# Weight chunks of a decoder trunk on their way to bf16: half-size casting loads held behind x, eight DRAM to DRAM conversions for four, no zero columns, half of the direct casts stored one period later

## The chip, the cores and the metric

The kernel runs on all 8 cores of one Trainium2 chip, each core with its own sequence of the batch and no traffic between cores. The metric is the device time in microseconds (us) of the slowest core. The weights are the same for all cores and each core converts and loads its own copy.

## The reference, cut to what matters

One layer: `h = x + W_out[concat(HGRN2(n), SWA(n))]` with `n = RMSNorm(x)`, then `h + SqReLU-MLP(RMSNorm(h))`, then a final RMSNorm, for 8 prompts of 4096 tokens and 128 samples of 8 tokens.

```python
zq, zf, zi, zg, sq, sk, sv = _split(xn @ w_in)          # 1024 -> 4*512 | 512, 128, 128
o_hg, S_new = _hgrn2(zq, zf, zi, zg, lb, hg_norm, S0)    # chunked linear recurrence, 4 heads of 128
o_swa, k_buf, v_buf = _swa_prompt(q, k, v, sinks)        # window of 128, 8 query heads, 2 kv heads
h = h + jnp.concatenate([o_hg, o_swa], axis=-1) @ w_out  # 1024 -> 1024
u = _rmsnorm(h, ln_mlp) @ w_up                           # 1024 -> 4096
h = h + jnp.square(jax.nn.relu(u)) @ w_down              # 4096 -> 1024
```

Inputs and weights are float32, matmuls run in bf16. So every weight has to be cast once and has to be on the core again for each group of tokens.

## The kernel before

**Groups and periods.** A core has 32 tiles of 128 tokens, in 8 groups of 4 tiles, and 16 samples of 8 tokens that ride along with group 3. For each group there is a *head* (`head_steps`, the input projections), a *back* (`back_steps`: recurrence and window attention, then the output projection and the norm of the MLP) and the MLP (`mlp_steps`). `interleave` weaves them: while the MLP of group g runs (a *period*), the back of group g+1 and the head of group g+2 are issued between its matmuls. Before the first period comes an opening: the head of group 0 (`head_steps` with `take=hold_on`), and then a *bridge*, in which `interleave("p", ...)` weaves the head of group 1 (on the buffers `A`) with the back of group 0.

**Weights.** The host packs the weights into 24 chunks of 1024 x 512, `wall` in DRAM (float32, 2 MB each). Chunk 0 is q, 1 is g, 2 is f, 3 the window queries s, 4 is v, 5 holds keys and values of the window attention in 256 columns and zeros in the other 256; 6 and 7 are W_out, 8 to 15 W_up, 16 to 23 W_down. On the core a chunk lies in one of five SBUF slots (`wring`, s_wr in the profile, 1 MB of bf16). `WORDER` is the order in which the slots are filled; it comes from two dry builds of the program and is `2 0 1 3 4 5 2 6 7 8 9 16 20 10 11 6 7 17 21 12 13 18 22 14 15 2 19 0 23 1 3 4 5 8 9 ...`. `w_prefetch` fills a slot as soon as it is released in the program's order; `w_load` does one load.

**The ways of a chunk.** All of them are DMAs:

- a *direct cast*, s_wr<-wall on the POOL queue, which reads float32 and writes bf16 into the slot;
- a *store*, wbf<-s_wr on the SP queue, which saves the bf16 chunk to DRAM (`wbf`) after a direct cast. `tick`, called at each step of the weaving, issues it ten steps or more later, or `w_load` does when the slot or the chunk is wanted;
- a *read*, s_wr<-wbf on the SP queue, 1 MB, for every later use;
- a *conversion*, wbf<-wall on the POOL queue, DRAM to DRAM, which `convert` issues during the bridge (`qc["conv"]`) every `tk["every"]` ticks for the next chunk of WORDER that isn't converted, at most two in flight, and each only when PE has reached the place of its issue.

SP and POOL work their queues in program order: a waiting DMA holds up all DMAs behind it. A direct cast waits until the cast before the last has landed (`casts[-2:-1]`); the first two wait instead for the tiles named in `hold_back`. In the head of group 0 the slots of chunks 0, 1, 3, 4 and 5 are held for the head of group 1; only the slot of f is released, and chunk 5 goes into it, once f is stored.

**The opening's order.** SP: four x tiles of group 0; then a wait for the third cast (`casts[2]`), four x tiles of group 1 (XR<-x); then the stores. `second_norms` makes the norms of group 1's tiles (`norm_pre` L554 to L565 on ACT and DVE, `norm_post` L572 transposes on PE and L574 on DVE); it is pulled, as `beside`, by the sections s and v of the head of group 0.

**Lines of the profile.** L583 is `fm_mm` (projections and W_up), L590 `tm_mm` (v and kv), L572 the transposes, L739 and L753 `hg_front`, L796 to L802 the recurrence, L830 and L855 the window attention, L881 its scores, L1011 the output projection, L1159 to L1181 the MLP's activation and W_down. L621, L627, L637 and L644 are ACT's ends of the projections (tanh, silu, copies), L888 the softmax's exp. L117 is the one line that issues every DMA, L73 the one line of every wait.

```python
for sec in order:                                  # head_steps, "fqgsvk"
    W, u = take(cid)
    ...
                        if beside is not None and sec == "s":
                            next(beside, None)
```

Of the kernel before, what the change touches and what calls it, by code (L numbers as in the profile page):

```python
# [14 lines left out]
G = 4  # L15
# [32 lines left out]
class Prog:  # L48
# [16 lines left out]
    def _wait(self, e, tok):  # L65
        if tok is None:
            return
        sn, v = tok
        if e is self.E["pe"] and sn == "e_pe":
            return  # L70
        if e.waited.get(sn, 0) >= v:
            return
        e.h.wait_ge(self.sems[sn], v)  # L73
        e.waited[sn] = v
# [92 lines left out]
def build_program(worder=None, weights=None):  # L167
# [193 lines left out]
    hold_back = []  # L361
    qc = {"conv": False}

    def store(one):
        cid, s_ = one[0], one[1]
        P.dma(wbf_d[cid], wring[s_].ap.rearrange("p a b -> p (a b)"), reads=[wring[s_]], writes=[wbfb[cid]],
              sem="ws%d" % s_)

# [4 lines left out]
    def w_load(l):  # L373
        cid = WORDER[l]
        for t_ in [t_ for t_ in stores if wslot_free[0] == t_[1] or t_[0] == cid]:
            stores.remove(t_)
            store(t_)
        s_ = wslot_free.pop(0)
        loaded[l] = s_
        dst = wring[s_].ap.rearrange("p a b -> p (a b)")  # L380
        if cid in converted:
            P.dma(dst, wbf_d[cid], reads=[wbfb[cid]], writes=[wring[s_]], sem="wr%d" % s_)
        else:
            converted.add(cid)
            e = P.E["pool"]
            for tok in [hold_back.pop(0)] if hold_back else casts[-2:-1]:
                P._wait(e, tok)
            casts.append(P.dma(dst, wall_d[cid], writes=[wring[s_]], sem="wc%d" % s_, q="pool"))
            stores.append([cid, s_, 10])

# [219 lines left out]
    def head_steps(parts, order="fqgsvk", take=w_use, give=w_release, beside=None):  # L610
# [55 lines left out]
        for sec in order:  # L666
            cid = cids[sec]
            W, u = take(cid)
            if sec in "fqgs":
                for h in range(4):  # L670
                    for B, _, _ in parts:
                        if sec == "f":
                            proj_f(W, B, h)
                        elif sec == "s":
                            proj_l(W, B, h)
                            half_gate()
                        else:
                            proj_s(W, B, h, B.qtT if sec == "q" else B.sgT)
                        if beside is not None and sec == "s":
                            next(beside, None)  # L680
                        yield W_DENSE * B.TB / 512
            elif sec == "v":
                for B, tiles, _ in parts:
                    for j, n in enumerate(tiles):
                        proj_v(W, B, j)
                        half_gate()
                        if beside is not None:
                            next(beside, None)
                        yield W_DENSE
            else:  # L690
                for B, tiles, _ in parts:
# [3 lines left out]
                    for j, n in enumerate(tiles):  # L695
                        proj_kv(W, B, j, n)
                        half_gate()
                        yield W_DENSE / 2
            past.add(sec)
# [543 lines left out]
    def main_schedule():  # L1243
# [73 lines left out]
        const_loads()  # L1317
        hold_back.extend([xs[0][0].w, xs[0][G - 1].w])
        const_ops()
# [3 lines left out]
        if casts:  # L1323
            w_prefetch(1)
            P._wait(P.E["sp"], casts[2])
        xs[1] = [load_x(n) for n in gtiles(1)]
        w_prefetch()
        xbs = []
# [22 lines left out]
        qc["conv"] = True  # L1351
        tk["every"] = 16
        tails = []
        given = []

        def give_up(u):
# [4 lines left out]
                                   take=lambda cid: held.pop(cid) if cid in held else w_use(cid), give=give_up),  # L1361
                   chain(back(0, iter(()), tails, lambda: len(given) >= 3), start_tail(tails)), 4, pace=1.25)
        qc["conv"] = False
        xq.extend([xt_load(xahead.pop(0)), xt_load(xahead.pop(0))])
        for g in range(NG):
# [80 lines left out]
```

How the kernel before makes its waits and increments, by code:

```python
    def _wait(self, e, tok):  # L65
        if tok is None:
            return
        sn, v = tok
        if e is self.E["pe"] and sn == "e_pe":
            return
        if e.waited.get(sn, 0) >= v:
            return
        e.h.wait_ge(self.sems[sn], v)
        e.waited[sn] = v
# [23 lines left out]
    def op(self, en, fns, reads=(), writes=()):  # L98
        e = self.E[en]
        if callable(fns):
            fns = [fns]
        self._deps(e, reads, writes)
        ins = None
        for f in fns:
            ins = f(e.h)
        ins.then_inc(self.sems[e.semname], 1)
        e.n += 1
        tok = (e.semname, e.n)
        self._mark(tok, reads, writes)
        return tok
# [1 line left out]
    def dma(self, out, in_, reads=(), writes=(), sem=None, q="sp"):  # L112
        e = self.E[q]
        sem = sem + "_" + q
        self.dsem(sem)
        self._deps(e, reads, writes)
        ins = e.h.dma_start(out=out, in_=in_)
        ins.then_inc(self.sems[sem], 16)
        self.dcnt[sem] += 16
        tok = (sem, self.dcnt[sem])
        self._mark(tok, reads, writes)
        return tok
```

## Time and profile before

| | us |
|---|---|
| median of 3 runs | 1644.03 |
| their lowest and highest | 1642.82, 1649.74 |
| the profiled execution's own time | 1645.24 |
| its span, core 4 (the slowest) | 1644.2 |
| its spans, all cores | 1628.2 to 1644.2 |

| engine | busy, share of the span |
|---|---|
| PE | 1514.3 us, 92% |
| ACT | 916.0 us, 56% |
| DVE | 736.8 us, 45% |
| POOL | 79.6 us, 5% |

The profile is of one execution on core 4. A matmul's row tells its own duration, about 0.38 us for 512 columns, and matmuls overlap in the pipeline: a group of 8 takes 1.73 us at the full clock. PEclk is the granted share of TensorE's full clock (2.4 GHz; 0.5 is the level of 1.2 GHz). "DMA share" is the mean busy share of the core's 16 DMA engines. The DMA queues: SP's are q1, POOL's q0, ACT's q10.

### The profile page before, as it was taken

To read this page: it belongs to the slowest core of one execution; us is meant where nothing else is said; L and a number is where in the kernel's file an instruction comes from. 1 tells how busy PE (TensorE), PEld (TensorE's weight loads), DVE (VectorE), ACT (ScalarE), POOL (GpSimd) and SP (SyncE) were. 2 spreads that over 40 slices of the span, in tenths; PEclk is the share of its full clock that TensorE was granted. 3 is DMA by queue.
4 is the path that set the end of the run, shared out by engine and by line. 5 is a ranking of instruction groups with operands and counts; after the bars stand their busy time and mean duration, and the time that the engine had idled before them with its cause. 6 is when DMAs were issued, how large, how long until landed. Compare 5 with 4: busy or idle time off the path is not lost.

```text
span 1644.2 us, 26297 instructions; the slowest of 8 cores (1628.2 to 1644.2 us)
## 1 busy us (share of the span) xinstructions
PE 1514.3 (92%) x8883; PEld 737.8 (45%) x8883; DVE 736.8 (45%) x1221; ACT 916.0 (56%) x1694; POOL 79.6 (5%) x154
## 2 busy tenths in 40 slices
PE   4778789899999988999999999999999999999997
PEld 2343344444444544444555544444445444444443
DVE  2545445335542546753544425553544425444222
ACT  3565545556557555546754576555655566444423
POOL 2000000000001001100000000000000000000000
PEclk9999999999999999999999999999999999999998
DMA  8965999966447266633633347734563345534541
GB/s 159 241 131 110 189 235 216 228 220 240 148 151 189 107 234 199 225 128 130 230 129 141 116 154 203 267 120 148 173 254 132 123 152 206 186 129 162 203 154 51
DMA packets 59362, 284.17 MB, mean 173 GB/s; under 512 B 10304, under 2 KB 19520, under 8 KB 32576
## 3 DMA queue, kind: packets, MB, share of 16 engines
q1 hardware_dynamic: 30400, 206.98, 36.7%
q0 software_dynamic: 19520, 70.26, 18.3%
q10 hardware_dynamic: 9312, 5.26, 1.2%
q8 instruction: 75, 1.23, 0.3%
q14 instruction: 55, 0.45, 0.1%
HBM read 265.69 MB, written 49.15 MB: 191 GB/s over the span
## 4 chain that ended last, share of the span: by engine, by line
PE 69%; DMA 12%; ACT 8%; DVE 5%; issue 5%; ACTq 0%; DVEq 0%; SPq 0%; POOL 0%; POOLq 0%
PE pb L583 32%; PE pb L1177 23%; PE pb L1011 6%; DMA s_wr<-wall 5%; DMA s_wr<-wbf 4%; PE pb L590 2%; ACT s_xnb L554 2%; ACT s_rl L1159 2%; PE pb L572 1%; DVE XR L1181 1%; DMA ss<-M 1%; DVE U L718 1%; DMA XR<-x 1%; PE pb L830 1%; PE pb L881 1%
## 5 line engine op out<-in xcount | busy, mean ns | idle before, releaser
L583 PE MATMUL pb<-s_hnT,s_wr 128*128 128x512 bf16 x2184 | 508.0, 382 | 14.4 <-DMA s_wr<-wbf 6.2
L1177 PE MATMUL pb<-s_wr,s_aT 128*128 128x512 bf16 x2048 | 476.7, 381 | 19.2 <-ACT s_aT L1162 15.5
L583 PEld LDWEIGHTS pb<-s_hnT,s_wr 128*128 128x128 bf16 x2184 | 207.9, 98 | 253.8 <-issue 29.6
L1177 PEld LDWEIGHTS pb<-s_wr,s_aT 128*128 128x128 bf16 x2048 | 194.7, 98 | 255.2 <-issue 44.0
L1181 DVE TENSOR_TENSOR XR<-pb,XR 128x512 f32<-128x512 f32 x256 | 175.5, 688 | 198.3 <-PE pb L1177 194.3
L1159 ACT ACTIVATE s_rl<-pb 128x512 bf16<-128x512 f32 (+1 forms) x288 | 159.8, 555 | 174.0 <-PE pb L583 170.6
L583 PE MATMUL pb<-s_xnT,s_wr 128*128 128x512 bf16 x952 | 223.8, 388 | 19.9 <-DMA s_wr<-wbf 11.4
L1162 ACT ACTIVATE s_aT<-s_rl 128x512 bf16<-128x512 bf16 x256 | 161.2, 630 | 24.4 <-ACT s_rl L1159 1.1
L583 PEld LDWEIGHTS pb<-s_xnT,s_wr 128*128 128x128 bf16 x952 | 92.9, 99 | 131.4 <-issue 31.2
L1011 PE MATMUL pb<-s_wr,s_omT 128*128 128x512 bf16 x512 | 123.2, 385 | 5.2 <-DMA s_wr<-wbf 4.2
L554 ACT ACTIVATE s_xnb<-XR 128x1024 bf16<-128x1024 f32 x72 | 75.9, 1054 | 90.3 <-DVE XR L1181 64.1
L565 DVE SCALAR_TENSOR_TENSOR s_xnb<-XR,s_rs,s_gmlp 128x1024 bf16<-128x1024 f32 x32 | 41.1, 1283 | 124.0 <-ACT s_rs L558 124.0
L888 ACT ACTIVATE U<-pb 128x512 bf16<-128x512 f32 x126 | 67.8, 590 | 38.7 <-PE pb L881 37.4
L1011 PEld LDWEIGHTS pb<-s_wr,s_omT 128*128 128x128 bf16 x512 | 50.0, 99 | 65.1 <-issue 8.6
L1201 DVE SCALAR_TENSOR_TENSOR XR<-XR,s_rs,s_gfin 128x1024 f32<-128x1024 f32 x32 | 41.1, 1285 | 81.9 <-ACT s_rs L558 79.5
L1014 DVE TENSOR_TENSOR XR<-pb,XR 128x512 f32<-128x512 f32 x64 | 44.0, 688 | 71.2 <-PE pb L1011 70.6
L572 PE MATMUL pb<-s_ident,s_xnb 128*128 128x128 bf16 x528 | 42.0, 225 | 35.2 <-DVE s_xnb L565 34.5
L590 PE MATMUL pb<-s_wr,s_xnT 128*128 128x512 bf16 (+2 forms) x448 | 65.4, 304 | 0.0
L565 DVE SCALAR_TENSOR_TENSOR s_xnb<-s_xt,s_rs,s_gmix 128x1024 bf16<-128x1024 f32 x25 | 32.1, 1284 | 67.5 <-ACT s_rs L558 67.5
L572 PEld LDWEIGHTS pb<-s_ident,s_xnb 128*128 128x128 bf16 x528 | 35.5, 100 | 51.3 <-issue 39.8
L117 POOL DMA_DIRECT2D y<-XR x32 | 17.3, 542 | 774.3 <-DVE XR L1201 423.1
L627 ACT ACTIVATE U<-pb 128x512 bf16<-128x512 f32 x56 | 33.2, 597 | 37.1 <-PE pb L583 36.1
(201 smaller groups left out, 1379.9 us busy)
## 6 DMA issues: line engine op xcount, KB each, us to landing
s_wr<-wbf SPq DMA_DIRECT2D x167, 1024.0 KB, 5.6
s_wr<-wall POOLq DMA_DIRECT2D x20, 1024.0 KB, 15.1
wbf<-s_wr SPq DMA_DIRECT2D x20, 1024.0 KB, 12.9
y<-XR POOLq DMA_DIRECT2D x32, 512.0 KB, 3.5
s_xt<-x POOLq DMA_DIRECT2D x20, 512.0 KB, 5.9
XR<-x POOLq DMA_DIRECT2D x20, 512.0 KB, 11.8
XR<-x SPq DMA_DIRECT2D x12, 512.0 KB, 10.6
wbf<-wall POOLq DMA_DIRECT2D x4, 1024.0 KB, 13.1
```

The lines of the kernel that those rows point to most:

```text
L554: P.op("act", lambda e: e.activation(out=scrap[:, :], in_=src[:, :], func=AF.Square, accum_out=ssq[:, 0:1]), reads=[src], writes=[ssq, scrap])
L565: P.op("dve", lambda e: e.scalar_tensor_tensor(out=xb[:, :], in0=src[:, :], scalar=rs[:, 0:1], in1=gain[:, :], op0=ALU.mult, op1=ALU.mult) ...
L572: P.op("pe", [lambda e, k=k: e.transpose(bkb[:, k * 128:(k + 1) * 128], xb[:, k * 128:(k + 1) * 128], C.ident[:, :]) for k in range(8)], r ...
L583: P.op("pe", [lambda e, k=k: e.matmul(bk[0:ncols, 0:TB], lhsT=W[:, k, col0:col0 + ncols], rhs=srcT[:, k, 0:TB], start=(k == 0), stop=(k == ...
L590: P.op("pe", [lambda e, k=k: e.matmul(bk[:, 0:ncols], lhsT=srcT[:, k, j * 128:(j + 1) * 128], rhs=W[:, k, c0:c0 + ncols], start=(k == 0), ...
L888: P.op("act", lambda e, pt=pt, bk=bk: e.activation(out=pt[:, :], in_=bk[:, :], func=AF.Exp, scale=0.125), reads=[bk], writes=[pt])
L1011: P.op("pe", [lambda e, k=k: e.matmul(bk[:, :], lhsT=B.omT[:, k, j * 128:(j + 1) * 128], rhs=W[:, k, :], start=(k == 0), stop=(k == 7)) fo ...
L1014: P.op("dve", lambda e: e.tensor_tensor(out=xs_[:, nh * 512:(nh + 1) * 512], in0=bk[:, :], in1=xs_[:, nh * 512:(nh + 1) * 512], op=ALU.add ...
L1159: P.op("act", lambda e, bk=bk, rl=rl, TB=TB: e.activation(out=rl[:, 0:TB], in_=bk[:, 0:TB], func=AF.Relu), reads=[bk], writes=[rl])
L1162: P.op("act", lambda e, fl=fl, rl=rl, TB=TB, B=B: e.activation(out=B.aT[:, fl, 0:TB], in_=rl[:, 0:TB], func=AF.Square), reads=[rl], writes ...
L1177: P.op("pe", [lambda e, f=f, B=B, j=j, W=W, bk=bk: e.matmul(bk[:, :], lhsT=B.aT[:, f, j * 128:(j + 1) * 128], rhs=W[:, f, :], start=(f == ...
L1181: P.op("dve", lambda e, nh=nh, bk=bk, xs_=xs_: e.tensor_tensor(out=xs_[:, nh * 512:(nh + 1) * 512], in0=bk[:, :], in1=xs_[:, nh * 512:(nh ...
```

## The change

It has these parts.

1. A direct cast is made as two DMAs of half a chunk each (rows 0 to 3 and 4 to 7 of the 8 blocks of 128). Each half waits until the half before the last has landed. A slot's reader waits for both halves (`_wait` takes a token of four parts).
2. The first half of the first cast waits for x tile 2 and the second half for x tile 3, where the first cast waited for tile 0 and the second cast for tile 3.
3. All five first casts are issued before group 1's x tiles, and SP waits for `casts[8]`, the first half of the fifth cast, before these tiles, not for the third cast.
4. Chunk 5 is cast, stored and read with its 256 used columns alone (`cut`), in runs of 256 elements.
5. `second_norms` is pulled in section k, once per tile, not in s and v.
6. The bridge has a lead of 0, not 4, and a conversion every 9 ticks, not 16: eight conversions for four (chunks 6, 7, 8, 9, 16, 20, 10, 11 for 6, 7, 8, 9).
7. After the bridge (`qc["thin"]`) every second direct cast isn't stored. Its chunk is cast directly once more in the next period, and stored then. There are ten first casts in the first period (of chunks 17, 21, 12, 13, 18, 22, 14, 15, 19, 23), where there were fourteen; 17, 12, 18, 14 and 19 are cast again in the second.

```diff
@@ -65,6 +65,9 @@
     def _wait(self, e, tok):
         if tok is None:
             return
+        if len(tok) > 2:
+            self._wait(e, tok[0:2])
+            tok = tok[2:]
         sn, v = tok
@@ -377,16 +380,32 @@
         s_ = wslot_free.pop(0)
         loaded[l] = s_
-        dst = wring[s_].ap.rearrange("p a b -> p (a b)")
         if cid in converted:
-            P.dma(dst, wbf_d[cid], reads=[wbfb[cid]], writes=[wring[s_]], sem="wr%d" % s_)
-        else:
-            converted.add(cid)
-            e = P.E["pool"]
+            P.dma(flat(wring[s_], cid), rows(wbf_d, cid), reads=[wbfb[cid]], writes=[wring[s_]], sem="wr%d" % s_)
+            return
+        e = P.E["pool"]
+        for half in range(2):
             for tok in [hold_back.pop(0)] if hold_back else casts[-2:-1]:
                 P._wait(e, tok)
-            casts.append(P.dma(dst, wall_d[cid], writes=[wring[s_]], sem="wc%d" % s_, q="pool"))
-            stores.append([cid, s_, 10])
+            casts.append(P.dma(flat(wring[s_], cid, half), rows(wall_d, cid, half), writes=[wring[s_]] if half == 0 else [],
+                               sem="wc%d_%d" % (s_, half), q="pool"))
+        wring[s_].w = casts[-2] + casts[-1]
+        if qc["thin"] and cid not in once and len(once) % 2 == 0:
+            once.append(cid)
+            return
+        once.append(cid)
+        converted.add(cid)
+        stores.append([cid, s_, 10])
+
+    def cut(ap, cid, half):
+        v = ap[:, 0:8, 0:256] if cid == 5 else ap
+        return v if half is None else v[:, 4 * half:4 * half + 4, :]
+
+    def flat(buf, cid, half=None):
+        return cut(buf.ap, cid, half)
+
+    def rows(dram, cid, half=None):
+        return cut(dram[cid].rearrange("p (a b) -> p a b", a=8), cid, half)
@@ -676,16 +695,12 @@
                             proj_s(W, B, h, B.qtT if sec == "q" else B.sgT)
-                        if beside is not None and sec == "s":
-                            next(beside, None)
                         yield W_DENSE * B.TB / 512
...
                         proj_v(W, B, j)
                         half_gate()
-                        if beside is not None:
-                            next(beside, None)
                         yield W_DENSE
@@ -695,6 +710,8 @@
                         proj_kv(W, B, j, n)
                         half_gate()
+                        if beside is not None:
+                            next(beside, None)
                         yield W_DENSE / 2
@@ -1315,16 +1332,15 @@
-        hold_back.extend([xs[0][0].w, xs[0][G - 1].w])
+        hold_back.extend([xs[0][G - 2].w, xs[0][G - 1].w])
         const_ops()
         w_prefetch(1)
         const_masks()
         w_prefetch(1)
         if casts:
-            w_prefetch(1)
-            P._wait(P.E["sp"], casts[2])
+            w_prefetch()
+            P._wait(P.E["sp"], casts[8])
         xs[1] = [load_x(n) for n in gtiles(1)]
-        w_prefetch()
@@ -1349,7 +1365,7 @@
         qc["conv"] = True
-        tk["every"] = 16
+        tk["every"] = 9
@@ -1359,8 +1375,9 @@
         interleave("p", head_steps([(A, gtiles(1), None)], order="qgsfvk",
                                    take=lambda cid: held.pop(cid) if cid in held else w_use(cid), give=give_up),
-                   chain(back(0, iter(()), tails, lambda: len(given) >= 3), start_tail(tails)), 4, pace=1.25)
+                   chain(back(0, iter(()), tails, lambda: len(given) >= 3), start_tail(tails)), 0, pace=1.25)
         qc["conv"] = False
+        qc["thin"] = True
```

What moves on the engines can't be read from the diff at three places. In what follows s_hnT is the buffer in which group 1's norms lie during the bridge, pb a PSUM bank. The first place is PE at the end of the head of group 0 and the start of the bridge. Before:

```order
L590 MATMUL pb<-s_wr,s_xnT 128x512 x8
L572 MATMUL pb<-s_ident,s_xnb 128x128 x8
L590 MATMUL pb<-s_wr,s_xnT 128x512 x24
L583 MATMUL pb<-s_xnT,s_wr 128x512 x8
L590 MATMUL pb<-s_wr,s_xnT 128x128 x32
L583 MATMUL pb<-s_hnT,s_wr 128x512 x32
L739 MATMUL pb<-U 128x128 x4
```

Now (lines are 16 to 19 higher: L602 is the old L583, L609 the old L590, L591 the old L572, L756 the old L739):

```order
L609 MATMUL pb<-s_wr,s_xnT 128x512 x32
L602 MATMUL pb<-s_xnT,s_wr 128x512 x8
L609 MATMUL pb<-s_wr,s_xnT 128x128 x16
L591 MATMUL pb<-s_ident,s_xnb 128x128 x8
L609 MATMUL pb<-s_wr,s_xnT 128x128 x8
L591 MATMUL pb<-s_ident,s_xnb 128x128 x8
L609 MATMUL pb<-s_wr,s_xnT 128x128 x8
L591 MATMUL pb<-s_ident,s_xnb 128x128 x16
L756 MATMUL pb<-U 128x128 x4
L770 MATMUL pb<-s_ident,U 128x128 x4
L602 MATMUL pb<-s_hnT,s_wr 128x512 x8
```

All four transposes of group 1 now stand behind the key projection, and the first recurrence step stands ahead of the q projection of group 1 (32 matmuls), not behind it.

The second place is the POOL queue from the fifth cast to the first cast of the first period. wc, ws, wr and cd are the semaphores of casts, stores, reads and conversions, with the slot's number; e_pe is PE's progress. Before:

```order
L117 DMA s_wr4<-wall 128x4096 [waits wc2_pool]
L117 DMA s_wr0<-wall 128x4096 [waits wc3_pool,e_pe,ws0_sp]
L117 DMA wbf<-wall 32x16384 [waits e_pe] x2
L117 DMA wbf<-wall 32x16384 [waits e_pe,cd0_pool]
L117 DMA wbf<-wall 32x16384 [waits e_pe,cd1_pool]
L117 DMA s_wr3<-wall 128x4096 [waits wc4_pool,wr3_sp,e_pe]
```

Now:

```order
L120 DMA s_wr4<-wall 128x2048 [waits wc3_0_pool]
L120 DMA s_wr4<-wall 128x2048 [waits wc3_1_pool]
L120 DMA s_wr0<-wall 128x4x256 [waits wc4_0_pool,e_pe,ws0_sp]
L120 DMA s_wr0<-wall 128x4x256 [waits wc4_1_pool]
L120 DMA wbf<-wall 32x16384 [waits e_pe] x2
L120 DMA wbf<-wall 32x16384 [waits e_pe,cd0_pool]
L120 DMA wbf<-wall 32x16384 [waits e_pe,cd1_pool]
```

The last two of these rows come three times each in a row, eight conversions in all, and the next direct cast is that of chunk 17, far into the first period. Chunk 5's cast waits for the store of f (ws0) as before.

The third place is the SP queue behind that store. Before:

```order
L117 DMA s_wr1<-wbf 128x4096 [waits cd0_pool,wr1_sp,e_pe]
L117 DMA s_wr2<-wbf 128x4096 [waits cd1_pool,wr2_sp,e_pe]
L117 DMA wbf<-s_wr3 128x4096 [waits e_pe,wc3_pool]
L117 DMA s_xt0<-x 128x1024
L117 DMA s_xt1<-x 128x1024
L117 DMA wbf<-s_wr4 128x4096 [waits e_pe,wc4_pool]
L117 DMA wbf<-s_wr0 128x4096 [waits e_pe,wc0_pool]
L117 DMA s_wr2<-wbf 128x4096 [waits wr2_sp]
```

Now:

```order
L120 DMA s_wr1<-wbf 128x4096 [waits cd0_pool,wr1_sp,e_pe]
L120 DMA s_wr2<-wbf 128x4096 [waits cd1_pool,wr2_sp,e_pe]
L120 DMA s_wr3<-wbf 128x4096 [waits cd0_pool,wr3_sp,e_pe]
L120 DMA s_wr4<-wbf 128x4096 [waits cd1_pool,e_pe,ws4_sp]
L120 DMA s_wr0<-wbf 128x4096 [waits cd0_pool,e_pe,ws0_sp]
L120 DMA s_xt0<-x 128x1024
L120 DMA s_xt1<-x 128x1024
L120 DMA s_wr1<-wbf 128x4096 [waits cd1_pool,wr1_sp,e_pe]
```

Both pieces begin with the reads of chunks 8 and 9. The four chunks behind them (16, 20, 10, 11) were direct casts with stores, and are now reads of 1 MB that wait for their conversions, and there is no store among them.

## Rows read from the trace of the kernel before

**Rows 1.** The page, chain that ended last, by line, whole span

```profile
PE pb L583 32%; PE pb L1177 23%; PE pb L1011 6%; DMA s_wr<-wall 5%; DMA s_wr<-wbf 4%; PE pb L590 2%; ACT s_xnb L554 2%; ACT s_rl L1159 2%; PE pb L572 1%; DVE XR L1181 1%; DMA ss<-M 1%; DVE U L718 1%; DMA XR<-x 1%; PE pb L830 1%; PE pb L881 1%
```

**Rows 2.** Windows: length; busy of PE, PEld, DVE, ACT, POOL; clock; DMA share; GB/s

```profile
89.00:146.00 57.00, 41.65 (x294) 21.03 (x293) 28.66 (x62) 41.40 (x61) 1.51 (x3) 0.91 0.64 121
...
172.00:212.00 40.00, 33.46 (x185) 15.56 (x183) 18.42 (x32) 20.58 (x39) 1.06 (x2) 0.91 1.01 219
212.00:317.00 105.00, 97.91 (x568) 47.18 (x567) 44.24 (x80) 55.38 (x102) 5.80 (x11) 0.97 0.99 230
317.00:346.00 29.00, 21.71 (x102) 9.69 (x101) 8.26 (x10) 15.31 (x23) 1.59 (x3) 0.88 0.71 204
346.00:500.00 154.00, 150.94 (x890) 73.02 (x888) 78.73 (x133) 88.92 (x166) 7.22 (x17) 1.00 0.51 180
```

**Rows 3.** PE's waits, 80 to 240 and 240 to 400 us: total, times, longest

```profile
PE pb L583 <- DMA s_wr<-wbf: 6.2, 1, 6.2
PE pb L1011 <- DMA s_wr<-wbf: 4.2, 1, 4.2
...
PE pb L583 <- DMA s_wr<-wbf: 7.3, 1, 7.3
```

**Rows 4.** The chain that ended last, 0 to 330 us: start, length, what

```profile
6.45 14.80 DMA s_wr<-wall
...
63.84 13.17 DMA s_wr<-wall
...
205.61 30.99 DMA s_wr<-wbf
...
318.53 13.98 DMA s_wr<-wbf
```

**Rows 5.** DMAs issued at 21.3, 42.5, 44.2, 61.9 and 92.6 us: last, us to landing

```profile
s_wr<-wall POOLq DMA_DIRECT2D x1, 1024.0 KB, 10.7
...
s_wr<-wall POOLq DMA_DIRECT2D x1, 1024.0 KB, 14.0
...
wbf<-s_wr SPq DMA_DIRECT2D x1, 1024.0 KB, 19.1
...
wbf<-s_wr SPq DMA_DIRECT2D x1, 1024.0 KB, 9.8
...
wbf<-wall POOLq DMA_DIRECT2D x1, 1024.0 KB, 12.8
```

**Rows 6.** DMAs issued in 212 to 317 and in 346 to 500 us

```profile
s_wr<-wall POOLq DMA_DIRECT2D x9, 1024.0 KB, 14.7
wbf<-s_wr SPq DMA_DIRECT2D x8, 1024.0 KB, 12.9
...
s_wr<-wbf SPq DMA_DIRECT2D x20, 1024.0 KB, 4.9
```

**Rows 7.** The page, DMA issues, whole span

```profile
y<-XR POOLq DMA_DIRECT2D x32, 512.0 KB, 3.5
```

**Rows 8.** PE timeline, 82 to 90 us: start, length

```profile
82.31 7.07 PE L583 MATMUL pb<-s_hnT,s_wr 128*128 128x512 bf16 x32
89.21 0.39 PE L739 MATMUL pb<-U 128*128 128x128 bf16 x4
```

**Rows 9.** ACT timeline, the norm of x tile 3 in the opening: start, length

```profile
20.93 1.06 ACT L554 ACTIVATE s_xnb<-XR 128x1024 bf16<-128x1024 f32 x1 [5.18 <-DMA XR<-x]
...
22.56 0.20 ACT L558 ACTIVATE s_rs<-s_tv 128x1 f32<-128x1 f32 x1
```

**Rows 10.** ACT's groups, 89 to 146 us: busy, mean ns of one

```profile
L627 ACT ACT_TABLE_LOAD x3 | 3.8, 1283 | 0.6 <-PE pb L583 0.6
L627 ACT ACTIVATE M<-pb 128x512 bf16<-128x512 f32 x5 | 3.0, 597 | 2.2 <-PE pb L583 2.2
```

**Rows 11.** Second period, timelines of SP's queue and PE

```profile
412.17 8.09 SPq L117 DMA_DIRECT2D s_wr<-wbf  x2
...
432.53 3.84 PE L1177 MATMUL pb<-s_wr,s_aT 128*128 128x512 bf16 x17
```

More of the change, by code:

```diff
@@ L361, in build_program @@
     hold_back = []
-    qc = {"conv": False}
+    once = []
+    qc = {"conv": False, "thin": False}
     def store(one):
         cid, s_ = one[0], one[1]
-        P.dma(wbf_d[cid], wring[s_].ap.rearrange("p a b -> p (a b)"), reads=[wring[s_]], writes=[wbfb[cid]],
-              sem="ws%d" % s_)
+        P.dma(rows(wbf_d, cid), flat(wring[s_], cid), reads=[wring[s_]], writes=[wbfb[cid]], sem="ws%d" % s_)
     def flush_stores():
```

## The prediction

> **What bounds the kernel now.** Start with the chain that ended last, grouped by line [rows 1]: PE's matmuls are most of it, but 5% is casting loads (s_wr<-wall) and 4% reads (s_wr<-wbf). PE is the bound; DMAs can only give back what PE waits for them. The windows [rows 2] say where. From 172 to 317 us the DMA engines are full (share 0.99 to 1.01) and TensorE's mean clock is 0.91 to 0.97; in the second period (346 to 500) the share is 0.51, the clock 1.00, and PE is busy for 150.94 of 154 us. So what the change can win lies in the first 346 us. There PE waits for reads three times, 6.2, 4.2 and 7.3 us [rows 3]. Each stall costs twice: the clock under 1.00 of these windows is the 1.2 GHz at which PE comes back after standing idle. The chain names the transfers: k's cast (63.84, 13.17 long) ends the opening at 77.0, and one read of 1 MB took 30.99 us, another 13.98 [rows 4], where 20 reads in the second period have a median of 4.9 [rows 6]. Reads are late because they share the engines with casts and stores.
>
> **The opening.** It ends when chunk 5 (k) has landed, since all that follows on PE hangs on it. Five casts run from 6.45 to 56.5 (the fifth, issued at 42.5, took 14.0) [rows 4, 5]: 50 us. Beside them ran group 1's x (2 MB) and f's store (1 MB), both issued from 42 on, because SP waited for the third cast. Under that load the store took 19.1 [rows 5], and k's cast stands behind it. Now SP waits for the ninth half (half of v), so nothing runs beside the casts but group 0's x. I begin the casts at about 9 (tile 2) and take 41 for them, 50 less the 9 or so that the 3 MB beside them cost (a 1 MB read alone takes 4.9 [rows 6], so 3 MB some 15, of which 9 fall before 56.5): v ends at 50, the ninth half at 46. Then store and x have the engines to themselves, but for three more stores. The store takes between 9.8 (the one issued at 61.9) and 19.1 [rows 5]; I take 14, so it ends at 60. For k's cast with half the bytes but shorter runs, beside the stores of q, g and s, I take 12. That is 72 for 77: **-5 us**. Bounds: 46 + 2.2 for issuing four x + 9.8 + 5.3 (half of 10.7, a cast with little beside [rows 5]) = 63.3, **-14**; 52 + 19.1 + 13.2 (the whole chunk's) = 84.3, **+7.5**. That the first cast waits for tile 2, not tile 0, costs nothing: PE can't start on f before tile 3's norm, 20.93 to 22.76 [rows 9], and x now comes without a cast beside it.
>
> **Behind k's landing** nothing is gained. Before, the rest of k and v and the q projection of group 1 (82.31, 7.07 long) fill 77.0 to 89.2, where the first recurrence step starts [rows 8]: 12.2 us. Now q stands behind that step, but the four norms of group 1 stand behind k on ACT. One takes from 20.93 to 22.76 [rows 9], 2.0 with its gap. So 1.7 (k's first projection) + 0.7 (its copy) + 4 x 2.0 + 1.4 (DVE's scaling) + 0.6 (transposes) = 12.4, the small terms rounded from single instructions of this kind: **0**.
>
> **Attention and tail.** From 89 to 146 the bridge hangs on ACT, busy for 41.40 of 57 us [rows 2]. A lead of 0 mixes its two parts otherwise: ACT switches its table 14 times in the bridge for 12, 1.28 us each, and four more tanh of group 1 (0.6 us each) come inside [rows 10]. All of it on the path, with one more switch, is 3 x 1.28 + 4 x 0.6 = 6.3; all beside it is 0. I take **+4**. The projections that were ahead stand in the tail: two groups of 8 matmuls of 1.73 at most, 0 to 3.5, **+2**. Two conversions are always in flight, 12.8 us each [rows 5]; where the first output projection wants chunk 7, its read shares with both: 0 to +5 (a read of 4.9 grown twofold), **+2**.
>
> **172 to 212.** Chunks 16, 20, 10 and 11 are reads now, not cast and stored, so the read of chunk 9, which cost 6.2, has no cast beside it. Gone are these 6.2 [rows 3] and the clock's share, 0.09 of 40 us = 3.6 [rows 2], 9.8 together. Conversions still run at the start of it: **-9**, bounds -10 to -4.
>
> **212 to 317.** Here were 9 casts with a median of 14.7 us and 8 stores with 12.9 [rows 6], at a share of 0.99. Now ten casts are left in the whole period, with 5 stores. The 4.2 us go, with the 30.99 us read behind them [rows 3, 4], and 0.03 of 105 us = 3.2 for the clock [rows 2]: **-7**, bounds -8 to 0.
>
> **317 to 346.** The 7.3 us come from the read of chunk 0, 13.98 us [rows 4] beside the cast of chunk 23. The cast stays, only a store leaves: **-1**, bounds -9 (7.3 and half of the clock's 0.12 of 29 us) to +3.
>
> **Second period.** Five chunks are cast again, each with a store. The read of chunk 17 issued at 412.17 is first used at 432.53 [rows 11], 20.4 us later; for all five it is 17.8 to 21.5. A cast of 10.7 fits, and the share of 0.51 leaves room, but a read behind it may be late: 0 to +6, **+2**. Nothing changes behind 500 us.
>
> **Sum**: -5 + 0 + 4 + 2 + 2 - 9 - 7 - 1 + 2 = **-12**. The profiled execution took 1645.2 us, 1.2 above the median of 1644.0, with a span of 1644.2 on core 4. Against its own time the sum gives 1633.2, against the median **1632.0**. Other cores have other stalls, and the fastest spans 1628.2 already, so the slowest core falls only as far as all lose theirs. Own range of this case: 1624 to 1640.
>
> **The rivals.** A measurement of this kernel can tell 0.5%, 8.2 us: below 1635.8 is faster, above 1652.3 slower.
>
> *More goes.* k lands at 72 - 6 = 66, and of the stall at chunk 0 with its clock 5 more go: **1621**. For it: a store alone took 9.8, half of 19.1. Against: the collision with chunk 23's cast is untouched.
>
> *No relief.* Eight conversions one after the other need until 89 + 8 x 13 = 193; the reads of 16 to 11 then wait for them, or the stalls come back at the casts of the period. Of the 16 for 172 to 317 only 7 are won: **1641**. For it: ten casts are the larger half of the old load. Against: while four conversions and attention ran, the share was 0.64 [rows 2].
>
> *Halves cost more.* y of 512 KB takes 3.5 us [rows 7], a read of 1024 KB 4.9 [rows 6]: half the size is 1.05 dearer than half the time, a chunk in halves 2.1. Five such chunks stand in the opening, 10.5: **1642.5**. Against: two halves are in flight at a time, which hides a fixed cost. The Trainium skill, "DMA: Bandwidth & Descriptors", section "Measured (HBM→SBUF, 128 partitions, SWDGE, issued from GpSimd)", asks for batches of at least 1 MiB for 75% of peak, and a half writes 512 KB; by that rule it would go as in this case, and the two rows agree in sign, for transfers one at a time.
>
> *Slower.* f's store stands behind a later wait of SP. If that lasts until 52, the store still takes 19.1 and k's cast 13.2, k lands at 84.3: 12.5 more than forecast; and if the gains of 172 to 317 halve (8 less), it is **1652.5**. It decides once k lands after 84. For it: both durations are rows. Against: the casts beside the store are over by then.
>
> **How the numbers follow.** Forecast 0.50, more goes 0.13, no relief 0.17, halves cost more 0.10, slower 0.10. Faster: three quarters of the forecast's case (1635.8 lies in the upper half of its range), all of "more goes", a quarter of "no relief": 0.38 + 0.13 + 0.04 = 0.55. Slower: half of the last, and 0.04 for the upper ends of the two before it: 0.09. The rest, 0.36, is the same. The range reaches from below 1621 to above 1642.5 and leaves out the slower case and the far ends: 1616 to 1647.
>
> **What would show it.** In the profile after: k's cast lands by 77 and the first recurrence step starts by 89; the attention of the bridge is 0 to 6 us longer, with 14 table loads; PE has no wait for s_wr<-wbf between 172 and 317, and the reads of 16, 20, 10 and 11 take 5 to 10 us; a stall of some 7 us at chunk 0 is still there; from 346 to 500 the clock is 1.00 and no wait for s_wr<-wall is over 2 us. The prediction is wrong if k lands after 84, if PE waits for a read of 16 to 11, or if a chunk that is cast again is late.

## The result, and the profile after

The changed kernel takes 1661.5 us (median of 6 runs), the kernel before 1643.2: the ratio is 1.0095, with a 95% interval of 1.0071 to 1.0119. By the ratio it is slower by 15.6 us, where 12 less were forecast, and outside the range of 1616 to 1647. The profiled execution took 1660.95, with a span of 1659.9 us on core 2 and 1642.4 to 1659.9 over the cores. (Two of the six runs, over 1830, had one die at a lower clock; all ratios and profiles below leave such runs out.)

PE's waits in the changed kernel (total, times, longest), core 2, for 0 to 80, 80 to 180, 240 to 400 and 400 to 560 us; they answer to [rows 3]:

```profile
PE pb L591 <- DVE s_xnb L584: 13.7, 4, 9.2
PE pb L602 <- DMA s_wr<-wall: 7.7, 3, 4.5
...
PE pb L602 <- DMA s_wr<-wall: 17.1, 1, 17.1
PE pb L1028 <- DMA s_wr<-wbf: 11.8, 2, 6.7
...
PE pb L602 <- DMA s_wr<-wbf: 7.3, 1, 7.3
...
PE pb L602 <- DMA s_wr<-wbf: 4.3, 1, 4.3
```

The stalls of 6.2 and 4.2 us are gone, the 7.3 us at chunk 0 stand. New are 17.1 us before the key projection, 11.8 at the first output projection and 4.3 in the second period. The windows (columns as in [rows 2]), cut at these places:

```profile
63.00:80.00 17.00, 0.03 (x1) 0.00 (x0) 3.84 (x6) 3.33 (x8) 1.49 (x2) 0.63 0.95 233
80.00:94.00 14.00, 9.39 (x73) 6.68 (x75) 7.64 (x11) 6.84 (x17) 0.00 (x0) 0.72 0.30 114
94.00:144.00 50.00, 36.42 (x251) 17.78 (x252) 23.88 (x53) 38.50 (x55) 2.51 (x5) 0.95 0.82 129
144.00:194.00 50.00, 36.52 (x202) 17.53 (x207) 20.68 (x31) 20.41 (x38) 1.48 (x3) 0.88 0.76 142
194.00:347.00 153.00, 139.93 (x802) 67.28 (x816) 67.59 (x117) 85.69 (x156) 12.20 (x23) 0.98 0.88 191
```

PE does nothing for 17 us, ACT and DVE little, and in the 14 us behind that PE's mean clock is 0.72. Behind that, 194 to 347 runs at 0.98 with a DMA share of 0.88, where the clock was 0.88 to 0.97 and the share mostly 0.99 [rows 2]: there the change wins as forecast.

**A common measure.** PE's semaphore counts the groups of matmuls that others wait for. The table has the time at which it reaches a count (*place*), the median of the eight cores of one profile, and two stretches: 116 to 290 is the difference of two such medians, 470 to 600 the median of the cores' own lengths. What each kernel is, stands in the next section. Place 34 lies behind the opening's end (with a lead of 4 the q projection of group 1 stands ahead of it, so only kernels of one lead compare there), 116 ends the bridge; from 116 on PE's program is the same in all.

| kernel | ratio (95%) | at 34 | at 116 | 116 to 290 | 470 to 600 |
|---|---|---|---|---|---|
| before | 1 | 84.4 | 173.4 | 161.5 | 125.6 |
| changed | 1.0095 (1.0071 to 1.0119) | 92.8 | 195.2 | 148.6 | 130.4 |
| lead4 | 1.0105 (1.0069 to 1.0141) | 96.8 | 194.0 | 144.4 | 130.0 |
| conv16 | 1.0041 (1.0009 to 1.0073) | 93.2 | 180.5 | 152.9 | 129.8 |
| nothin | 1.0105 (1.0056 to 1.0154) | 92.2 | 192.9 | 152.5 | 125.2 |
| full | 1.0094 (1.0073 to 1.0115) | 91.0 | 191.8 | 147.6 | 129.8 |
| spwait | 1.0077 (1.0058 to 1.0096) | 87.6 | 188.4 | 148.0 | 130.6 |
| beside_old | 1.0010 (0.9987 to 1.0032) | 79.2 | 180.7 | 147.5 | 125.3 |
| open_old | none (two runs count) | 79.5 | 181.6 | 147.5 | 125.3 |
| phase2 | 1.0045 (1.0009 to 1.0080) | 92.4 | 193.2 | 148.2 | 125.4 |
| before_k | 1.0083 (1.0058 to 1.0108) | 98.4 | 188.6 | 159.6 | 125.6 |
| old_conv16 | 0.9941 (0.9920 to 0.9961) | 79.3 | 165.2 | 150.6 | 125.3 |
| best_halves | 0.9936 (0.9913 to 0.9958) | 79.8 | 165.8 | 156.0 | 125.3 |
| best_full | 0.9897 (0.9844 to 0.9949) | 76.6 | 162.0 | 152.2 | 125.2 |
| best_full2 | 0.9935 (0.9912 to 0.9959) | 77.4 | 163.8 | 152.8 | 125.2 |
| best_lead4 | 0.9973 (0.9937 to 1.0009) | 81.0 | 170.3 | 156.5 | 125.6 |
| best_nothin | 0.9937 (0.9891 to 0.9983) | – | – | – | – |
| best_nothin2 | 0.9944 (0.9924 to 0.9963) | 78.1 | 163.8 | 159.8 | 125.2 |

So the change is: +21.8 up to the bridge's end, -12.9 in 116 to 290, +4.8 in 470 to 600, 13.7 together; the median span rose by 14.2 (1638.2 to 1652.4). In 116 to 290 the cores of the kernel before differ by themselves, from 153.5 to 165.3 us (changed: 143.6 to 149.5); the median of their own lengths falls by 11.0.

### The profile page after: what moved, and what is told of

Same layout as the page of the kernel before. It is cut to its first block, busy times and chain, and to the rows that moved or that the text cites. A ratio compares the mean times of both kernels' runs of the same rounds, so it can differ in the third digit from the quotient of the medians.

```text
span 1659.9 us, 26203 instructions; the slowest of 8 cores (1642.4 to 1659.9 us)
## 1 busy us (share of the span) xinstructions
PE 1503.9 (91%) x8713; PEld 737.2 (44%) x8883; DVE 736.7 (44%) x1221; ACT 917.6 (55%) x1696; POOL 94.3 (6%) x180
## 4 chain that ended last, share of the span: by engine, by line
PE 70%; ACT 9%; DMA 8%; issue 6%; DVE 5%; another core or an unknown queue 1%; ACTq 0%; DVEq 0%; SPq 0%; POOL 0%; POOLq 0%
PE pb L602 33%; PE pb L1194 23%; PE pb L1028 6%; DMA s_wr<-wbf 4%; ACT s_rl L1176 2%; ACT s_xnb L573 2%; DMA s_wr<-wall 2%; PE pb L609 2%; PE pb L591 1%; DVE U L735 1%; DMA ss<-M 1%; DVE XR L1198 1%; PE pb L898 1%; PE pb L847 1%
## 5 line engine op out<-in xcount | busy, mean ns | idle before, releaser
L602 PE MATMUL pb<-s_hnT,s_wr 128*128 128x512 bf16 x2125 | 497.8, 381 | 11.4 <-ACT U L776 2.5
L1194 PE MATMUL pb<-s_wr,s_aT 128*128 128x512 bf16 x1986 | 469.7, 382 | 26.3 <-ACT s_aT L1179 18.2
L602 PEld LDWEIGHTS pb<-s_hnT,s_wr 128*128 128x128 bf16 x2184 | 207.2, 98 | 243.1 <-issue 17.7
L602 PE MATMUL pb<-s_xnT,s_wr 128*128 128x512 bf16 x928 | 221.7, 390 | 45.8 <-DMA s_wr<-wall 24.8
L1176 ACT ACTIVATE s_rl<-pb 128x512 bf16<-128x512 f32 (+1 forms) x288 | 159.6, 554 | 166.8 <-PE pb L602 159.7
L602 PEld LDWEIGHTS pb<-s_xnT,s_wr 128*128 128x128 bf16 x952 | 93.2, 100 | 157.4 <-issue 57.2
L1028 PE MATMUL pb<-s_wr,s_omT 128*128 128x512 bf16 x494 | 123.1, 389 | 13.7 <-DMA s_wr<-wbf 11.8
L1218 DVE SCALAR_TENSOR_TENSOR XR<-XR,s_rs,s_gfin 128x1024 f32<-128x1024 f32 x32 | 41.1, 1284 | 81.9 <-ACT s_rs L577 79.5
L591 PE MATMUL pb<-s_ident,s_xnb 128*128 128x128 bf16 x528 | 42.5, 227 | 26.9 <-DVE s_xnb L584 25.2
L609 PE MATMUL pb<-s_wr,s_xnT 128*128 128x128 bf16 (+2 forms) x447 | 65.8, 305 | 0.8 <-DMA s_wr<-wall 0.4
L591 PEld LDWEIGHTS pb<-s_ident,s_xnb 128*128 128x128 bf16 x528 | 35.7, 101 | 42.0 <-issue 30.9
```

What stands on the lines that cost most here:

```text
L591: P.op("pe", [lambda e, k=k: e.transpose(bkb[:, k * 128:(k + 1) * 128], xb[:, k * 128:(k + 1) * 128], C.ident[:, :]) for k in range(8)], r ...
L602: P.op("pe", [lambda e, k=k: e.matmul(bk[0:ncols, 0:TB], lhsT=W[:, k, col0:col0 + ncols], rhs=srcT[:, k, 0:TB], start=(k == 0), stop=(k == ...
L609: P.op("pe", [lambda e, k=k: e.matmul(bk[:, 0:ncols], lhsT=srcT[:, k, j * 128:(j + 1) * 128], rhs=W[:, k, c0:c0 + ncols], start=(k == 0), ...
L1028: P.op("pe", [lambda e, k=k: e.matmul(bk[:, :], lhsT=B.omT[:, k, j * 128:(j + 1) * 128], rhs=W[:, k, :], start=(k == 0), stop=(k == 7)) fo ...
L1176: P.op("act", lambda e, bk=bk, rl=rl, TB=TB: e.activation(out=rl[:, 0:TB], in_=bk[:, 0:TB], func=AF.Relu), reads=[bk], writes=[rl])
L1194: P.op("pe", [lambda e, f=f, B=B, j=j, W=W, bk=bk: e.matmul(bk[:, :], lhsT=B.aT[:, f, j * 128:(j + 1) * 128], rhs=W[:, f, :], start=(f == ...
```

## The experiments

**One part undone at a time, first four.** lead4: the bridge's lead of `0` becomes `4`. conv16: `tk["every"] = 9` becomes `16`. nothin: `qc["thin"] = False`. open_old:

```diff
-            w_prefetch()
-            P._wait(P.E["sp"], casts[8])
+            w_prefetch(1)
+            P._wait(P.E["sp"], casts[5])
         xs[1] = [load_x(n) for n in gtiles(1)]
+        w_prefetch()
...
+                        if beside is not None and sec == "s":
+                            next(beside, None)
...
                         proj_v(W, B, j)
                         half_gate()
+                        if beside is not None:
+                            next(beside, None)
...
                         proj_kv(W, B, j, n)
                         half_gate()
-                        if beside is not None:
-                            next(beside, None)
```

> The changed kernel with the bridge's lead at 4 again, all else as changed. In the changed kernel the bridge ends about 21 us later than before, and PE waits some 12 us for the read of chunk 7 at the first output projection (core 2: 11.8 us in two waits, core 4: 12.8 us in one). Theory A, slots: with a lead of 0 the q projection of group 1 runs inside the bridge, the slot of q is given up some 18 us later, and the reads of chunks 2, 6 and 7 behind it come late. Then a lead of 4 brings the read of chunk 7 back before 130 us, the wait is under 4 us, and the time falls by 9 to 13, to about 1650. Theory B, contention: the read takes 20 us because two conversions are in flight, whatever the lead. Then the wait stays at 6 us or more and the time falls by less than 5, to about 1658.

> The changed kernel with a conversion every 16 ticks again (four conversions, the chunks 16, 20, 10, 11 direct casts again). Theory A, slots: the read of chunk 7 is still issued near 136 us, wanted near 143, and PE still waits at least 3 us. Theory B, contention: the read takes about 5 us, PE waits less than 2 us and the bridge ends 12 to 16 us earlier than in the changed kernel. By both theories some stalls come back behind 172 us, 4 to 10 us; so A gives 1662 to 1668, B 1650 to 1656.

> The changed kernel with every first direct cast stored, so that none is cast again in the second period. Theory: the casts in the second period cost what the trace shows between the PE places at 487 and 622 us, 2 to 9 us more than before (126 us then), by a store of chunk 19 that holds up three reads on SP. Then this kernel gives these back, has a wait or two more of up to 4 us in 212 to 317, and comes to 1655 to 1660. Rival: the stores in the first period cost more than the second casts, and the time is 1662 or more.

> The changed kernel with the opening's order of before: SP waits for the third cast (its second half) and not for the ninth half, the last two chunks are cast behind group 1's x, and the norms of group 1 are pulled in s and v. Halves, tiles 2 and 3 for the first cast, 256 columns, lead, conversions and thinning stay as changed. Theory A: the later wait of SP costs the opening, since f's store is issued at 54 and lands at 66, and behind k (landed near 80) come the four norms on ACT. Then k lands at 70 to 75, the first recurrence step starts at or before 84 instead of 92 to 94, and the time falls by 6 to 10, to about 1653. Rival: the opening is bound by the bytes of the casts, k lands at 78 to 80 again, and the time falls by less than 3.

lead4 gives nothing in time: place 116 at 194.0 for 195.2, ratio 1.0105. Theory A (slots given up late) wanted the read of chunk 7 to be issued before 130 us and the wait gone. It is issued at 134.7 for 136.4 (medians of the cores), so the lead isn't what makes it late. But 194.0 is the middle of two groups of four cores. In four the read takes 22.1 to 22.6 us, PE waits 11.3 to 12.0 for it, and place 116 stands at 200.4 to 202.4; in the other four it takes 9.3 to 10.7, no wait is left, and place 116 stands at 184.1 to 187.5. What the read meets differs from core to core, which speaks for theory B, contention; why these four cores are spared stays open. Theory B's own "the wait stays" came true on half of the cores.

conv16 reaches 116 at 180.5, 14.7 us earlier, and pays back 4.3 in 116 to 290. PE's wait for W_out is gone (0.3 us on one core is all). That is theory B. The reads show it. First the changed kernel's read of chunk 7, issued at 136.8; then the DMAs that conv16 and old_conv16 issue in 119 to 145 us:

```profile
s_wr<-wbf SPq DMA_DIRECT2D x1, 1024.0 KB, 20.7
```

```profile
wbf<-wall POOLq DMA_DIRECT2D x2, 1024.0 KB, 14.8
s_wr<-wbf SPq DMA_DIRECT2D x2, 1024.0 KB, 10.6
```

```profile
s_wr<-wbf SPq DMA_DIRECT2D x2, 1024.0 KB, 6.2
wbf<-wall POOLq DMA_DIRECT2D x1, 1024.0 KB, 10.6
```

Beside two conversions the read takes 20.7 us. PE waits 11.8 us for it and for chunk 6's. All cores agree: chunk 7's read takes 17.8 to 21.3 us in the changed kernel, 4.9 to 7.4 in conv16, 4.8 to 8.2 in old_conv16 and 4.8 to 5.9 before. With four conversions in the bridge it comes in time. nothin is as slow as the changed kernel (1.0105): it has 125.2 us in the second period, as before, and 3.9 more in 116 to 290. open_old was the surprise: place 34 13.3 us earlier, expected were 8 to 10. Its two times that count (1636.05 and 1644.94) are too few for a ratio.

**The two halves of the opening.** spwait has the first piece of that diff alone, beside_old the rest. old_conv16 is open_old with conversions every 16 ticks. full casts whole chunks:

```diff
-        for half in range(2):
+        for half in (None,):
...
-            P._wait(P.E["sp"], casts[8])
+            P._wait(P.E["sp"], casts[4])
```

> The changed kernel with one part of the opening undone: SP waits for the third cast again (its second half) and the last two chunks are cast behind group 1's x. The norms of group 1 stay in section k. open_old, with both undone, brought the first recurrence steps about 13 us forward (PE place 34: median of the cores 79.5 for 92.8). Theory A, the late store of f: most of it comes from the wait, by k's cast, which lands near 70; place 34 then stands at 83 to 86 and the time falls by 6 to 10. Theory B, the norms: k lands as early, but the four norms on ACT behind it still take 12 to 14 us and place 34 falls by less than 5, to 88 or more; the time falls by less than 5.

> The changed kernel with the other part undone: the norms of group 1 are pulled in s and v again, while SP still waits for the ninth half. Theory A: k lands near 80 as in the changed kernel, but nothing but k's own projection stands behind it, so place 34 stands at 84 to 87, and the time falls by 6 to 8. Theory B: x of group 1 lands at 57 to 63 now, so PE stalls in sections s and v for the transposes, 5 us or more; f's store and k's cast are not affected, and since PE is idle for 17 us before k lands anyway this costs nothing. Both together give 1653 to 1656; a time above 1659 would say that the norms' place is not what costs.

> Opening as before (as in open_old) and four conversions (as in conv16); halves, 256 columns, a lead of 0 and thinning stay. If the two parts add up: from open_old (1636 to 1645 in its undisturbed runs) 13 us go in the bridge and 4 come back in 212 to 317, so 1628 to 1634, faster than the kernel before. If instead the stall of the bridge needs only one of the two causes to go (PE comes early or reads are quick), the time stays at 1636 or more.

> The changed kernel with direct casts of whole chunks again, all else as changed (SP waits for the fifth cast, the last before k's). By the traces two halves of 1 MB read take 7 to 9 us each with two in flight, as fast as whole chunks. Theory: halves are neither dearer nor cheaper; SP's wait ends 1 to 4 us later (the tenth half instead of the ninth), and the time moves by less than 4 us: 1658 to 1666. Rival, halves cost more (2 us a chunk): the opening is 5 us or more shorter with whole chunks and the time is below 1656.

beside_old takes back 13.6 us at place 34 and its ratio is 1.0010: the norms' place, not SP's wait, is the main cause, and by about twice what its theory A gave (6 to 9 us at place 34, 6 to 8 in time); theory B's "costs nothing" holds for the new stall in s and v. With the norms in s and v, SP's wait costs nothing (79.2 with it, 79.5 without); with them in k, undoing it gives 5.2 (spwait, 87.6). The traces show how the two meet (core 2 of the changed kernel, core 0 of beside_old, the slowest of each). In the changed kernel f's store (issued at 54.1) and then the two casts of k (at 67) take:

```profile
wbf<-s_wr SPq DMA_DIRECT2D x1, 1024.0 KB, 12.3
...
s_wr<-wall POOLq DMA_DIRECT2D x2, 256.0 KB, 11.9
```

and in beside_old (issued at 52.3 and 64):

```profile
wbf<-s_wr SPq DMA_DIRECT2D x1, 1024.0 KB, 11.0
...
s_wr<-wall POOLq DMA_DIRECT2D x2, 256.0 KB, 7.3
```

A store goes to SP when PE has passed its place. Without transposes to wait for, PE ran through s and v and was done at 63; so the stores of q, g and s were issued at 55.6, 56.2 and 59.8 and ran beside f's store and k's casts. In beside_old PE waits for a norm of group 1 in between,

```profile
PE pb L591 <- ACT s_tv L575: 8.7, 1, 8.7
```

so q's store goes at 54.1, but g's at 64.9 and s's at 71.2, and k lands at 73.4 for 79.9. These are the slowest cores; the medians of the eight are 72.8 and 77.4, 4.6 apart. Then ACT, in the changed kernel:

```profile
83.81 0.58 ACT L663 CAST s_kT_all<-pb 128x512 bf16<-128x512 f32 x1 [16.20 <-remote]
84.29 1.06 ACT L573 ACTIVATE s_xnb<-XR 128x1024 bf16<-128x1024 f32 x1
...
91.19 0.20 ACT L577 ACTIVATE s_rs<-s_tv 128x1 f32<-128x1 f32 x1
```

ACT was idle for 16.20 us, with group 1's x landed since 63.5, and the four norms stood in its program behind k's copy. PE's rows of the changed kernel and of beside_old:

```profile
80.14 3.15 PE L602 MATMUL pb<-s_xnT,s_wr 128*128 128x512 bf16 x7 [17.11 <-DMA s_wr<-wall]
...
87.66 0.89 PE L591 MATMUL pb<-s_ident,s_xnb 128*128 128x128 bf16 x8 [2.65 <-DVE s_xnb L584]
...
93.91 0.39 PE L756 MATMUL pb<-U 128*128 128x128 bf16 x4
```

```profile
74.31 1.89 PE L602 MATMUL pb<-s_xnT,s_wr 128*128 128x512 bf16 x8
76.04 1.95 PE L609 MATMUL pb<-s_wr,s_xnT 128*128 128x128 bf16 x32
79.35 0.38 PE L758 MATMUL pb<-U 128*128 128x128 bf16 x4 [1.35 <-DVE s_vS_all L671]
```

From k's landing to the first recurrence step it is 14.0 us in one, 5.9 in the other (medians of the cores: 14.1 and 6.2, so 7.9 of the 13.6 us lie here), in part since PE came back from 17.11 us of idleness at 1.2 GHz (7 matmuls in 3.15 us for 8 in 1.89). beside_old's PE still waits 10.9 to 14.1 us for W_out, and its place 116 is at 180.7. old_conv16 takes that away too: place 116 at 165.2, ratio 0.9941, faster than the kernel before as expected. full had a ratio of 1.0094: halves neither save nor lose what a ratio can tell here.

**A store's place, and the parts of the faster kernel.** phase2 adds one line behind `qc["thin"] = True`: `tk["i"] += 2`. The other three are old_conv16 with `qc["thin"] = False` (best_nothin), with the lead of 4 (best_lead4) and with whole chunks (best_full, where SP waits for `casts[2]`).

> The changed kernel with 2 added to the counter of ticks when the bridge ends, and nothing else. A store goes out only at a tick whose number divides by 3; in the kernels with the norms in section k the store of chunk 19 (cast again in the second period) stands on SP ahead of the reads of chunks 0 and 23, in those with the norms in s and v behind both. The stretch between the PE places 470 and 600 takes 130 us (median of the cores) in the first, 125.3 in the second, as before. Theory: that one position is the 5 us; SP waits there until the cast has landed, and the reads behind it come late. Then the stretch takes 125 to 126 here and the time falls by 3 to 8. Rival: the stretch is longer because of when the second casts run beside the samples' cache loads, which move with the opening's length; then it stays at 129 to 131.

> old_conv16 (ratio 0.994 to before) with every first direct cast stored, none cast again. Theory: thinning wins in the first period (in the changed kernel the stretch 246 to 290 took 3.5 us less with it) and costs nothing in the second where the store order is right (125.3 us). So without it the stretches up to place 290 take 3 to 8 us more in sum, as 14 casts all have stores, and the ratio is 0.996 to 0.999. Rival: thinning does nothing when the reads have their slack; ratio within 0.002 of 0.994.

> old_conv16 with the bridge's lead at 4. Theory A: the lead of 0 is what wins in the opening, since the q projection of group 1 (7 us of PE) no longer stands between k and the first recurrence step and fits into the bridge, which ACT bounds. Then place 116 stands 3 to 7 us later than in old_conv16 (165.2) and the ratio is 0.996 to 0.999. Theory B: the bridge is as much shorter as the opening is longer (as between the changed kernel and lead4, where place 116 stood at 195 and 194); then the ratio is 0.993 to 0.995.

> old_conv16 with direct casts of whole chunks. In full, the changed kernel with whole chunks, the ratio was the same as with halves (1.0094 for 1.0095). Theory A: halves do nothing here either, the ratio is 0.993 to 0.996. Theory B: with the opening's old order, halves let the third cast and so f's store and k's cast go out earlier, which they can't where nine halves are waited for; then place 34 stands 2 us or more later here than 79.3 and the ratio is 0.996 or more.

phase2's stretch takes 125.4 for 130.4, as its theory said and against its rival: a store's position was the 5 us. Its ratio, 1.0045 for 1.0095, was taken on another chip, and the intervals overlap. SP's queue in the changed kernel, then in phase2:

```profile
496.41 0.32 SPq L120 DMA_DIRECT2D s_wr<-wbf  x1
520.16 0.32 SPq L120 DMA_DIRECT2D wbf<-s_wr  x1
520.60 8.22 SPq L120 DMA_DIRECT2D s_wr<-wbf  x4
```

```profile
499.85 21.81 SPq L120 DMA_DIRECT2D s_wr<-wbf  x3
523.94 0.32 SPq L120 DMA_DIRECT2D wbf<-s_wr  x1
524.37 0.37 SPq L120 DMA_DIRECT2D s_wr<-wbf  x1
```

In the first, no read is issued for 24 us; the store of chunk 19 waits for its cast (landed at 517.55), and four reads stand behind it. In the second, two of them go first. Two other stores moved by one position each, near 268 and 468 us; neither lies in this stretch, and 116 to 290 is the same (148.2 for 148.6). The norms' place moved the count of ticks, and with it this store: the kernels with thinning and the norms in k take 129.8 us or more here, those with the norms in s and v 125.2 to 125.6. best_lead4 reaches 116 at 170.3, 5.1 later than old_conv16: theory A, but its ratio overlaps. best_full reaches 34 at 76.6 for 79.3; its ratio is lower, but it was taken on another chip than old_conv16; the next part has both on one chip. best_nothin's ratio, 0.9937 for 0.9941, is the one its rival gave: without thinning nothing is lost that a ratio can tell, where 3 to 8 us were expected.

**Both sides, on one chip.** before_k is the kernel before with the norms moved to k (the last two pieces of open_old's diff and the one of section s, reversed). best_halves, best_full2 and best_nothin2 are old_conv16, best_full, and best_full without thinning.

> The kernel before with one edit: the norms of group 1 are pulled in section k instead of s and v. Theory: this edit alone costs the opening, by two ways: PE runs faster through s and v, so the stores of q, g and s reach the DMA engines while f's store is still under way, and k's cast lands 3 to 7 us later; and four norms on ACT stand between k and the q projection of group 1. Between beside_old and the changed kernel place 34 moved by 13.6 us (79.2 to 92.8), 20 us in time with the store's place on SP. Expected here: place 34 at 94 to 99 for 84.4, time up by 8 to 14, ratio 1.005 to 1.009. Rival: with a lead of 4 and the old order of casts the norms hide behind PE's other work, ratio under 1.003.

> The kernel of old_conv16 once more, beside best_full2 and best_nothin2 on the same chip: opening's order, norms' place and number of conversions as before; halves, 256 columns, lead 0 and thinning as changed. Expected: ratio 0.992 to 0.996, place 34 at 79 to 80.

> The kernel of best_full once more: the same as best_halves with direct casts of whole chunks. In the traces of the two, v had landed at 61.8 with halves and at 53.4 with whole chunks, k at 75.8 and 71.1. If halves cost what these show, place 34 is 2 to 3 us earlier than with halves, 246 comes another 2 to 4 earlier, and the time is 3 to 7 us less: ratio 0.988 to 0.992. If that was chance, the two agree within 2 us.

> best_full2 with every first direct cast stored, none cast again. If thinning is worth what the stretches of best_nothin show (176 to 246 and 246 to 290: 56.8 and 55.5 us for 53.2 and 51.3 in old_conv16), the time is 5 to 9 us more than best_full2's. If the stores fit beside the casts, within 2 us.

before_k alone costs 0.83%, within the 0.5 to 0.9% expected, with place 34 at 98.4 for 84.4, 14.0 us, near the 13.6 between the changed kernel and beside_old. Its PE waits 14.6 us for k:

```profile
PE pb L572 <- DVE s_xnb L565: 20.5, 4, 8.9
PE pb L583 <- DMA s_wr<-wall: 14.6, 1, 14.6
```

On this core k landed at 77.1, as on core 4 before (77.0): f's store landed earlier, at 60.2, but k's cast, with the stores of q, g and s now beside it, took 16.5 for 13.17 [rows 4]. Over the cores k landed at 77.2 for 74.3 (medians), 2.9 later; 3 to 7 were expected. From there to the first recurrence step it is 23.9 us for 12.2: 11.7 of the 14.0 are the norms behind k. The other three agree: 1633.8, 1634.0 and 1634.7 us, for 1643.6 before. The 3 to 7 us expected of whole chunks and the 5 to 9 of thinning didn't come. Whole chunks bring place 34 forward by 2.4 us, as in the first pair (2.7), and thinning takes 7.0 us off 116 to 290 between two single profiles (148.4 to 159.0 us on the cores with it, 152.3 to 166.1 without), but neither shows in the time, which the slowest of eight cores sets. They stay unresolved. Parts 2 and 4 of the change (tiles 2 and 3, the 256 columns) were never undone by themselves; what they are worth is not shown.

## Why the prediction was wrong

- **The opening, -5 us**: wrong in sign. k landed at 79.9 for the 72 forecast and the 77.0 of before (medians of the cores: 77.4, before 74.3). The step that failed is "I begin the casts at about 9 (tile 2) and take 41 for them": tile 2 landed at 11.4, the casts ran from 12.1 to 55.7, and SP's wait ended at 51.6, not 46. Issuing four x tiles took another 2.5 us, which stood in the bounds and not in the sum. The store (12.3 for 14) and k's casts (13.5 from the store's landing, for 12) were near. So 5.6 + 2.5 - 1.7 + 1.5 is the miss of 7.9. (The bounds and the slower rival have small slips: 84.3 is 7.3 above 77.0 and 12.3 above 72, not 7.5 and 12.5.) And "but for three more stores" took the stores as given in time, though they hang on PE: with the norms in s and v, two of them came after k's cast had begun, and k landed at 73.4 (beside_old).
- **Behind k's landing, 0**: the working was near (12.4, measured 14.0, the rest a slow clock), but it netted two parts of opposite sign. The lead of 0 would have made it 5.9; the norms took 8 back. The failed step is to price the sum against before, and not to ask what each part does alone: the norms' place was a term of +8 put at nothing.
- **Attention, tail and chunk 7, +8** (4 + 2 + 2): from the first recurrence step to place 116 core 2 took 102.4 us, core 4 before 85.5: +16.9. The step that was mis-sized is "its read shares with both: 0 to +5": a read of 4.9 grew fourfold, to 20.7, and PE waited 11.8 us for reads of W_out. The trace of before had a read of 30.99 us [rows 4], under casts and stores; I took twice the second period's median instead. Undoing the four extra conversions gives back 14.7 of the 16.9 (conv16).
- **172 to 346, -17**: right in mechanism. 116 to 290 fell by 12.9; no read wait is left but the 7.3 at chunk 0, as forecast, though the reads of 16, 20, 10 and 11 took 8.7 to 17.8 us, not 5 to 10. The eight conversions are worth 4.3 of it (conv16), for a price of 14.7 in the bridge, and thinning 3.9 (nothin).
- **Second period, +2**: +4.8, within its bounds, but by a store's place on SP and not by slow casts.
- **Halves, 0, and their rival (+10.5)**: 1.8 to 2.7 us at place 34, nothing in the ratio. The Trainium skill, "DMA: Bandwidth & Descriptors", section "Measured (HBM→SBUF, 128 partitions, SWDGE, issued from GpSimd)", asks for batches of at least 1 MiB; the opening agrees in sign (whole chunks are earlier by 1.8 to 2.7 us), at a sixth to a fourth of what the rival made of it.
- **The slower rival** (0.10, 1652.5) was the nearest: f's store behind SP's later wait. Of its numbers the wait until 52 came true (51.6) and the cast of 13.2 nearly (13.5), but the store took 12.3, not 19.1, so its point, k after 84, was not reached. The price came from the norms and the conversions, for which I had no rival, so its nearness in time is luck.

## What to carry to other kernels

Work that fills an engine's idle time before a late transfer costs nothing; the same work behind that transfer costs its whole length, and the wait it filled becomes idle time at a slower clock afterwards. Where DMAs are issued when an engine passes a place, moving work off this engine moves the DMAs too: list who starts earlier, and what it meets. When background transfers are made denser, look for the read with the least slack in their reach and price it with a row of that kind under load, not with the median. Look at all cores before a median is trusted: lead4's hid two groups 15 us apart. And undo the parts one at a time: here two of seven, the norms' place (14 us of the opening) and the density of the conversions (15 us of the bridge), each cost about as much as the change as a whole, and with these two and SP's wait undone the rest was 0.6% faster than before.

## What was not expected of the hardware

A read of 1 MB took 4.9 us in a calm stretch (median) and 20.7 beside two conversions, while the conversions themselves went only from 12.8 [rows 5] to 15.3 and 18.7: the read paid most of the sharing. And after 17.1 us of idleness PE ran 7 matmuls in 3.15 us, and its 8 transposes at 87.66 still in 0.89, where those at 91.47 took 0.61: the granted clock was 1.2 GHz until 84.4, 2.4 until 87.8, 1.2 once more until 91.2 and 2.4 behind it (0.72 in the mean of 80 to 94). PE had waited 2.65 us for a norm in between, so the work broken by short waits fell back to 1.2 GHz once.
